# One over the root mean square: a power of -1/2 on GpSimd behind an Identity on ScalarE, in place of a logarithm and an exponential on ScalarE

## What is computed

```
def rmsnorm(u, g):
    uf = u.astype(jnp.float32)
    y = uf * lax.rsqrt(jnp.mean(uf * uf, axis=-1, keepdims=True) + EPS)
    return (y * g.astype(jnp.float32)).astype(u.dtype)
```

## Time and profile before

| | us |
|---|---|
| median of 3 runs | 4126.52 (4120.57 to 4128.76) |
| the profiled execution | 4124.59 |
| its span | 4123.3 |
| TensorE busy | 3896.6 |
| VectorE busy | 2200.1 |
| ScalarE busy | 1483.2 |
| GpSimd busy | 494.0 |

### The profile page before, as it was taken

One profiled execution on the slowest core, in us unless ns is written; L12 is line 12 of the kernel. 1 busy time (PEld: TensorE's weight loads), 2 busy tenths in 40 slices (PEclk: granted clock), 3 DMA queues, 4 the chain that ended last, 5 costly groups with the idle time before them and its releaser, 6 DMA issues.

```text
span 4123.3 us, 48859 instructions
## 1 busy us (share of the span) xinstructions
PE 3896.6 (95%) x20254; PEld 3107.3 (75%) x20254; DVE 2200.1 (53%) x3857; ACT 1483.2 (36%) x1865; POOL 494.0 (12%) x748
## 2 busy tenths in 40 slices
PE   6998989999999889999899999999997999999999
PEld 4755778888775578876778878878876888888887
DVE  2275553333547464464544356778863666654444
ACT  3245532122234632234553432444443322222222
POOL 0000000000000000000002000457664111100000
PEclk9999999999999899999999999999998999999999
DMA  5410113323120022231114233355455656643332
GB/s 184 156 38 1 62 43 122 123 104 121 72 74 1 21 82 92 102 130 65 62 42 145 75 121 118 123 169 178 140 174 186 196 182 191 190 137 120 114 123 82
DMA packets 109838, 459.84 MB, mean 112 GB/s; under 512 B 9216, under 2 KB 43120, under 8 KB 68912
## 3 DMA queue, kind: packets, MB, share of 16 engines
q1 hardware_dynamic: 82048, 354.96, 24.2%
q0 software_dynamic: 27568, 101.74, 8.3%
HBM read 389.04 MB, written 67.63 MB: 111 GB/s over the span
## 4 chain that ended last, share of the span: by engine, by line
PE 80%; DVE 9%; ACT 5%; DMA 3%; issue 2%; POOL 2%; SPq 0%; DVEq 0%; ACTq 0%; POOLq 0%
PE ps L591 22%; PE ps L592 22%; PE ps L593 22%; DMA gdram<-GST 1%; PE ps L2612 1%; DVE ACC L1436 1%; PE ps L1235 1%; PE ps L502 1%; PE ps L670 1%; DVE WL L473 1%; DVE MX L1409 1%; POOL Y L2748 1%; PE ps L2159 1%; PE ps L1314 1%; PE ps L2386 1%
## 5 line engine op out<-in xcount | busy, mean ns | idle before, releaser
L591 PE MATMUL ps<-HH,WH 128*128 128x512 f32 x2760 | 1058.2, 383 | 50.7 <-DVE HL L897 21.1
L592 PE MATMUL ps<-HL,WH 128*128 128x512 f32 x2760 | 1044.8, 379 | 0.0
L593 PE MATMUL ps<-HH,WL 128*128 128x512 f32 x2760 | 1041.6, 377 | 0.0
L473 DVE TENSOR_TENSOR WL<-stage,WH 128x2048 fp32r<-128x2048 f32 x246 | 562.9, 2288 | 428.6 <-ACT WH L462 428.6
L462 ACT ACTIVATE WH<-stage 128x2048 fp32r<-128x2048 f32 x246 | 469.1, 1907 | 555.5 <-PE ps L593 493.7
L591 PEld LDWEIGHTS ps<-HH,WH 128*128 128x128 f32 x2760 | 524.8, 190 | 161.4 <-issue 48.0
L593 PEld LDWEIGHTS ps<-HH,WL 128*128 128x128 f32 x2760 | 523.2, 190 | 103.8
L592 PEld LDWEIGHTS ps<-HL,WH 128*128 128x128 f32 x2760 | 524.9, 190 | 98.5 <-issue 1.2
L591 PE MATMUL ps<-AHp,WH 128*128 128x512 f32 x1024 | 406.1, 397 | 7.7 <-ACT Y L2930 7.6
L592 PE MATMUL ps<-ALp,WH 128*128 128x512 f32 x1024 | 405.5, 396 | 0.0
L593 PE MATMUL ps<-AHp,WL 128*128 128x512 f32 x1024 | 405.5, 396 | 0.0
(11 more groups left out here) (420 smaller groups left out, 4968.2 us busy)
## 6 DMA issues: line engine op xcount, KB each, us to landing
stage<-in_w SPq DMA_DIRECT2D x64, 1024.0 KB, 4.8
stage<-in_u SPq DMA_DIRECT2D x64, 1024.0 KB, 4.8
stage<-in_v SPq DMA_DIRECT2D x64, 1024.0 KB, 4.8
stage<-in_w_mod SPq DMA_DIRECT2D x48, 1024.0 KB, 4.8
GR<-gdram POOLq DMA_DIRECT2D x32, 1024.0 KB, 8.0
adram<-GR SPq DMA_DIRECT2D x22, 1024.0 KB, 3.9
AR<-adram POOLq DMA_DIRECT2D x88, 256.0 KB, 3.5
gdram<-GST SPq DMA_DIRECT2D x16, 1024.0 KB, 5.7
```

Source lines behind the costliest of these rows:

```text
L473: dve.e.tensor_tensor(k.WL[o % 2][:, 0:w], k.stage[n % 2][:, 0:w], k.WH[o % 2][:, 0:w].bitcast(F32), ALU.subtract).then_inc(*dve.done("sla ...
L591: pe.e.matmul(o, wh[:, kk, cs], L.hh[:, kk, z], start=first, stop=False)
L592: pe.e.matmul(o, wh[:, kk, cs], L.hl[:, kk, z], start=False, stop=False)
L593: mm = pe.e.matmul(o, wl[:, kk, cs], L.hh[:, kk, z], start=False, stop=last)
```

## The change

ScalarE's logarithm becomes an Identity with the same scale and bias, which leaves the mean square plus EPS in `RS`. The exponential on ScalarE is left out; in its place GpSimd raises `RS`, in place, to the power -1/2, with the exponent broadcast from a column that a memset fills at the start. The powers of 768 columns are x, kvn (twice), qn, conf, br6, br4 and att of layer 0; those of 512 columns are qn, conf, br6, br4 and att of layer 1, 18 heads, and p; kc has 31. GpSimd does them at the head of, or between, its DMA issues. PSUM buffers are given back at the Identity, as before at the logarithm. The calls in `scalar_z`, `scalar_att`, `scalar_mix` and `scalar_queries` change from `scalar_rstd` to `scalar_mean`. The event of the other norms is renamed.

```
...
+    k.minus_half = new("minus_half", [128, 1])
...
-def scalar_rstd(k, act, name, n, D, segs, ring, *ends):
-    scalar_rstd_log(k, act, name, n, D, segs, ring, *ends)
-    scalar_rstd_root(k, act, name, segs)
...
+def scalar_mean(k, act, name, n, D, segs, ring, *ends):
...
     act.wait_ge("stat", (name, n - 1))
-    act.e.activation(r[:, a:b], p[:, a:b], ACT.Ln, bias=k.epsc[:, 0:1], scale=1.0 / D).then_inc(*act.done("rstd_ln", name))
+    act.e.activation(r[:, a:b], p[:, a:b], ACT.Identity, bias=k.epsc[:, 0:1], scale=1.0 / D).then_inc(
+        *act.done("mean_sq", name))
...
-def scalar_rstd_root(k, act, name, segs):
+def pool_rstd(k, pool, name, segs):
     a, b = span(segs)
     r = k.RS.of(name)
-    act.wait_ge("rstd_ln", name)
-    act.e.activation(r[:, a:b], r[:, a:b], ACT.Exp, scale=-0.5).then_inc(*act.done("rstd", name))
+    pool.wait_ge("mean_sq", name)
+    pool.e.tensor_tensor(r[:, a:b], r[:, a:b], k.minus_half[:, 0:1].broadcast_to([128, b - a]), ALU.pow).then_inc(
+        *pool.done("rstd", name))
...
@@ pool_start
     pool.e.dma_start(k.sinM[:, :], io["sinM"]).then_inc(*pool.landed("sinM"))
+    pool.e.memset(k.minus_half[:, :], -0.5).then_inc(*pool.done("exponent", 0))
+    pool.wait_ge("exponent", 0)
+    pool_rstd(k, pool, ("x", 0), [LAT, CTX])
...
@@ scalar_z
             for name, D, segs, end in rows:
-                scalar_rstd_log(k, act, name, 1 if D == 128 else 2, D, segs, k.psum, end)
-            for name, D, segs, end in rows:
-                scalar_rstd_root(k, act, name, segs)
+                scalar_mean(k, act, name, 1 if D == 128 else 2, D, segs, k.psum, end)
...
@@ pool_att
+    pool_rstd(k, pool, ("kvn", l), [LAT, CTX])
+    pool_rstd(k, pool, ("qn", l), both(l))
     pool.wait_ge("roped", (l, "k"))
...
     pool.e.dma_start(k.WQ[:, :, :], io["w_q_b"][l]).then_inc(*pool.landed(f"wq{l}"))
+    for name in ("conf", "br6", "br4", "att"):
+        pool_rstd(k, pool, (name, l), both(l))
...
@@ scalar_rope_roots
         act.wait_ge("bones", key)
-        act.e.activation(r[:, 0:n], p[:, 0:n], ACT.Ln, bias=k.epsc[:, 0:1], scale=1.0 / 64).then_inc(*act.done("rope_ln", key))
+        act.e.activation(r[:, 0:n], p[:, 0:n], ACT.Identity, bias=k.epsc[:, 0:1], scale=1.0 / 64).then_inc(*act.done("rope_mean", key))
+
+
+def pool_rope_roots(k, pool, keys):
+    n = 31 if keys and keys[0][0] == "kc" else 512
     for key in keys:
         r = k.RS.of(key)
-        act.wait_ge("rope_ln", key)
-        act.e.activation(r[:, 0:n], r[:, 0:n], ACT.Exp, scale=-0.5).then_inc(*act.done("rope_rstd", key))
+        pool.wait_ge("rope_mean", key)
+        pool.e.tensor_tensor(r[:, 0:n], r[:, 0:n], k.minus_half[:, 0:1].broadcast_to([128, n]), ALU.pow).then_inc(
+            *pool.done("rope_rstd", key))
...
@@ pool_heads
+    for i in range(0, 6, 2):
+        pool_rope_roots(k, pool, N_HEADS[i:i + 2])
+    pool_rope_roots(k, pool, [("kc",)])
     pool.wait_end("compress", "pe", "act", "dve")
...
@@ pool_dheads
             key = d_head(hp, i)
+            if i % 2 == 0:
+                pool_rope_roots(k, pool, [key, d_head(hp, i + 1)])
             pool.wait_ge("rope_add", key)
...
@@ pool_queries
+    pool_rstd(k, pool, ("p", 0), [LAT])
     pool.wait_end("merge", "pe", "act", "dve")
...
```

More of the change, by code:

```diff
@@ L39 @@
     "mod_products": ("mod_mm", "mod_col"),
-    "rms_rows": ("square", "rstd_ln", "xx", "rstd", "root1", "root2"),
+    "rms_rows": ("square", "mean_sq", "xx", "rms_spread", "root1", "root2"),
+    "pool_roots": ("rstd", "rope_rstd", "exponent"),
     "sums": ("moments", "rows_mm"),
     "att_evicted": ("k_head", "q_head", "v", "p_exp", "p_turned", "o_out", "sum_rows", "silu"),
-    "heads_evicted": ("kvc", "rope_raw", "rope_sq", "rope_ln", "rope_rstd", "vsw", "gate_rows", "gate", "dv", "hid_rows", "hid", "kz", "vcm"),
+    "heads_evicted": ("kvc", "rope_raw", "rope_sq", "rope_mean", "vsw", "gate_rows", "gate", "dv", "hid_rows", "hid", "kz", "vcm"),
     "sparse_evicted": ("bs_exp", "ptc", "ns_exp", "ns_turned", "yn"),
@@ L655, in tensor_stat_sum @@
     ring = ring or k.psum
-    p, t = ring.take(pe, ("stat", name), ("rstd_ln", name)), k.TA.of((name, 7))
+    p, t = ring.take(pe, ("stat", name), ("mean_sq", name)), k.TA.of((name, 7))
     pe.wait_ge("sq_sum", (name, 7))
@@ L672, in tensor_stat @@
     if c == n - 1 and not keep:
-        ring.give(("stat", name), ("rstd_ln", name))
-def scalar_rstd(k, act, name, n, D, segs, ring, *ends):
-    scalar_rstd_log(k, act, name, n, D, segs, ring, *ends)
-    scalar_rstd_root(k, act, name, segs)
-def scalar_rstd_log(k, act, name, n, D, segs, ring, *ends):
+        ring.give(("stat", name), ("mean_sq", name))
+def scalar_mean(k, act, name, n, D, segs, ring, *ends):
     a, b = span(segs)
@@ L831, in tensor_rows @@
 def tensor_rows(k, pe, names, i, segs):
-    p, t = k.psum.take(pe, ("rows", names[i]), ("rstd", names[i])), k.TA.of(("roots", names[0]))
+    p, t = k.psum.take(pe, ("rows", names[i]), ("rms_spread", names[i])), k.TA.of(("roots", names[0]))
     pe.wait_ge(("inverse1", "inverse2")[i], names[0])
@@ L859, in scalar_roots @@
             i = act.e.activation(r[:, s0:s0 + sn].rearrange("p (q n) -> p q n", q=4), rows[:, :, s0 // 4:(s0 + sn) // 4], ACT.Copy)
-        i.then_inc(*act.done("rstd", name))
+        i.then_inc(*act.done("rms_spread", name))
 def vector_roots(k, dve, names, segs, xx, ss):
@@ L902, in scaled @@
         t = k.TD.take(dve, (y, c), ("x_new", (y, c)))
-        dve.wait_ge("rstd", y)
+        dve.wait_ge("rms_spread", y)
         for (s0, sn) in segs:
@@ L918, in vector_add_norm_split @@
         u = k.TD.take(dve, (x, c), ("norm_lo", (x, c)))
-        dve.wait_ge("rstd", x)
+        dve.wait_ge("rms_spread", x)
         dve.wait_ge("x_new", (y, c))
@@ L1041, in scalar_z @@
     else:
-        scalar_rstd(k, act, ("x", 0), 8, 1024, [LAT, CTX], k.psum, norm_end(("x", 0), 8, [LAT, CTX]))
+        scalar_mean(k, act, ("x", 0), 8, 1024, [LAT, CTX], k.psum, norm_end(("x", 0), 8, [LAT, CTX]))
         r, p = k.RS.take(act, "xx", ("xx_kept", 0)), k.psum.of(("stat", ("x", 0)))
@@ L1293, in tensor_att @@
         elif u[0] == "root":
-            k.psum.give(("stat", (u[1], l)), ("rstd_ln", (u[1], l)))
+            k.psum.give(("stat", (u[1], l)), ("mean_sq", (u[1], l)))
     pe.mark(f"att{l}")
@@ L1379, in scalar_att @@
             end = ("conf_normed", (l, 1)) if u[1] == "conf" else ("branch", (l, int(u[1][2])))
-            scalar_rstd(k, act, (u[1], l), 2, 256, segs, k.psum, end)
+            scalar_mean(k, act, (u[1], l), 2, 256, segs, k.psum, end)
         elif u[0] == "silu":
@@ L1551, in scalar_mix @@
             act.e.activation(k.HH[:, c, z], k.Y[:, c, z], ACT.Copy).then_inc(*act.done("m_hi", (l, c, s0)))
-    scalar_rstd(k, act, ("att", l), 4, 512, segs, k.psum, norm_end(("att", l), 4, segs))
+    scalar_mean(k, act, ("att", l), 4, 512, segs, k.psum, norm_end(("att", l), 4, segs))
     scalar_norm_split(k, act, ("att", l), 4, segs, None, k.HH)
@@ L1730, in tensor_rope @@
     if step == 2:
-        p, t = k.psn.take(pe, ("bones", key), ("rope_ln", key)), k.TA.of(key)
+        p, t = k.psn.take(pe, ("bones", key), ("rope_mean", key)), k.TA.of(key)
         pe.wait_ge("rope_sq", key)
@@ L2563, in scalar_queries @@
 def scalar_queries(k, act):
-    scalar_rstd(k, act, ("p", 0), 8, 1024, [LAT], k.psn, norm_end(("p", 0), 8, [LAT]))
+    scalar_mean(k, act, ("p", 0), 8, 1024, [LAT], k.psn, norm_end(("p", 0), 8, [LAT]))
     scalar_norm_split(k, act, ("p", 0), 8, [LAT], None, k.HH2, o2_linear(k).end)
```

## The result

The changed kernel takes 6957.1 us (median of 4 runs, 6955.9 to 6959.8) where the kernel before, run beside it, takes 4123.6 us (4119.8 to 4128.8): a ratio of 1.687, 95% interval 1.685 to 1.689. The forecast was 4315 us with a range up to 4720. The direction was right, and the size was far off.

A forecast was written before the change was run, and what follows sets the result against it. TensorE, busy 95% of the span, was taken as the bound, with ScalarE counting only where TensorE waits. Exposed powers 15 + 17 + 34 + 17 + 98 + 9 = 190 us on 4124.6 gave 4315 us, range 4105 to 4720.

The forecast's parts named there:

- two loads return: ScalarE, one table load per layer before the first softmax, covered by a row-maximum wait: costed at nothing, 2.6 us otherwise.
- the chain GpSimd, VectorE, TensorE: Heads: VectorE's scaling waits for GpSimd some 18 us a pair longer, TensorE's rotation for VectorE about 12 us a pair.
- the size at x and p: First and last roots, where VectorE already waits: power less the ScalarE load and exponential saved, +15 us at x, +9 at p.
- the price: One GpSimd power: five passes, 22 ns a column, 11.4 us for 512 columns and 17.0 us for 768.
- a simple pass: Lower bound of the power, from GpSimd's line 2748 with two operations: 4.5 ns a column, 2.4 us for 512, 3.5 for 768.
- dearer than ten passes: Rival: dependent operations on GpSimd; every further 22 ns a column adds 405 us, 5530 us at 88 ns; chance 0.17.
- the cover: Time from the Identity's end to when the root is wanted, subtracted from each power as its budget, place by place.
- the first three pairs: Of nine head pairs, budgets to TensorE's rotation (5.1 us for the first); all nine together were to lose +98 us.
- kvn and qn: Two powers in a row per layer; VectorE stands, TensorE's ready products cover part: +5 us in layer 0, +12 in layer 1.
- the row maxima: Attentions: VectorE holds the next units' row maxima while waiting for the root; +34 us in layer 0, +17 in layer 1.
- Wrong in kind: Sign against the prediction: VectorE's own instructions get longer while GpSimd computes, which no earlier row would explain.
- The floor: Rival: the power costs what a simple pass costs and TensorE's waits behind ScalarE's roots go: -14 us, 4110 us, chance 0.20.

The follow-up runs named there:

- the multiplication's run: Changed kernel with each GpSimd power replaced by a multiplication with the same -1/2, 1/rms left out: 4093.7 us, 0.992 of the kernel before.
- the forecast's own price: Changed kernel with powers on only 70 of 512 and 105 of 768 columns, 11.6 and 17.1 us each: 4416.1 us, 1.070 of the kernel before.
- the exchange of order: The 70 and 105 column run with window-attention softmax pieces ahead of the heads' scaling in VectorE's list: 4376.2 us, against 4416.1 without.
- the split: Changed kernel with its eight 768-column powers issued as 512 and then 256 columns, nothing left out: 6960.3 us in one run.
- one table: Kernel before, logarithm and exponential kept on ScalarE but from one table set loaded ahead of the wait: 4084.3 us, ratio 0.990.

## Why the prediction was wrong

*Right:* that the power stands in the path; that ScalarE's Identity costs the logarithm's time, without a load; that two loads return; that GpSimd's queue and the hand-off cost nothing that shows (the multiplication's run); the chain GpSimd, VectorE, TensorE; the size at x and p.

*The step that failed first* is the price: "a logarithm, a product and an exponential ... some twenty operations; in ten passes of two that is 45 ns a column", of which it took half. The power takes 159 ns a column, 7 times the forecast's 22 and 3.5 times its upper end. What the bound leaned on, a simple pass, does hold for a simple operation (a multiplication of 512 columns takes 1.04 us), but it says nothing of a power, which took as long as 79 of them. It is the term that put the result out of the range; the chance of 0.17 for "dearer than ten passes" was the true case, and its count, every further 22 ns a column 405 us, gives 190 + (159 - 22)/22 x 405 = 2712 us, 4124.6 + 2712 = 6837, against 6957 measured; what is left, 120 us, is about the 101 us that the second step and the slower products of layer 1's MLP make up. The estimate of 34 us for 512 columns from the rule of 4 cycles (the Trainium skill, "GPSIMD Engine Reference", section "Performance pitfalls for Q7 kernels") was nearer than the forecast's 11.4 and still short of the 82.0.

*The step that failed second* is the cover. At the forecast's own price it is most of the error of 101 us; some 10 us of that are the slower products of layer 1's MLP, for which the prediction had no term. "The budget counted from the end of the Identity to the moment when the result is wanted" took the use of that result alone, the rotation or the normed branch. But VectorE works through one list, and what is late first is what it has queued next: a softmax piece in the heads, 40 us as the exchange of order shows. In the first three pairs, which have no such pieces behind them, the same budgets hold (17.7, 5.7 and 15.3 us lost where 23.0 less the budget gives 17.9, 4.1 and 14.2). At kvn and qn the text named the queued split and then let TensorE's ready products cover it; in the trace at the forecast's price TensorE waits 16.0 us in layer 1 for just that split (line 475), and in layer 0 13.5 us for the instruction that VectorE has right behind the scaling (line 1472). That the row maxima play the same part in the attentions is by the order of the lists; it wasn't tried.

*Wrong in kind*, by the prediction's own test, since VectorE's instructions did get longer (2200.1 to 2442.8 us busy); but the split shows that this cost nothing.

*The floor* (-14 us) was too small: -32 with a multiplication (with the 10 us lost in layer 1's MLP), -44 with one table (without them). The loads weighed more on the path than the waits of TensorE that the prediction named; that a later root also delays what stands behind it on VectorE would explain it, but was not tried by itself.

## What to carry to other kernels

Before an operation is moved to another engine, measure that very operation there, by itself, at two widths; here a multiplication and a power of the same columns differ by a factor of 79. Count the budget of a result not to its own use but to the first instruction that is queued behind that use on the waiting engine, whatever it belongs to. And when the thing to be rid of is a table load, look first for a set that holds both functions, and load it by hand ahead of the wait.

## What was not expected of the hardware

A power on GpSimd costs the same for 1 partition as for 128 (81.90 and 81.91 us for 512 columns), and the same for exponents of -1/2, 1.0 and 2.0.

While GpSimd runs one power of 768 columns, a VectorE instruction that has two inputs in SBUF stands for as long as 512 of them take (82 us), and a float32 copy in SBUF until the power's end (102.6, 122.7 and 163.5 us under 640, 768 and 1024 columns). Under a power of 512 columns the hold is 0.7 us (1.14 us for a copy of 0.43). With the powers issued as 512 and 256 columns, the scaling of kv is held by 0.8 us (1.79 against 1.01). The Trainium skill, "SBUF — State Buffer", section "Who interferes with whom", says that such VectorE instructions and a GpSimd instruction that reads SBUF take a pair of ports in turns, each for its whole length. The instructions that were held here are of these kinds; the length the runs show otherwise: not the whole power where it has 512 columns, and for two inputs not the whole power where it has 768.
